# An encoder layer whose first stage is put in another order: x is transposed at once, shift and scale become columns, two engines share their sum

## Chip, cores and metric

One core of one Trainium2 chip. The time is the device time of one launch in microseconds (us), from a few runs of the same program; smaller is better. The profile is one more execution of it, taken with the hardware profiler.

## What is computed

One layer of a bidirectional encoder on 512 tokens of width 1024, all in fp32. Cut to what matters here:

```python
mod = silu(c) @ w_ada + b_ada                     # c: (1, 1024), w_ada: (1024, 6*1024)
sh_a, sc_a, g_a, sh_f, sc_f, g_f = split(mod, 6)
h = layer_norm(x) * (1.0 + sc_a) + sh_a           # (512, 1024)
proj = h @ w_in                                   # w_in: (1024, 3072): q, k, v of two head groups
o_na = neighbourhood_attention(proj, na_rpb)      # 8 heads, learned 2-D relative bias
o_diff = diff_attention(proj, t5_bias, lambda)    # 4 heads, two softmax maps, T5 bucketed bias
x = layer_norm(ALPHA * x + (1.0 + g_a) * (concat(o_na, o_diff) @ w_out), ln1)
h = layer_norm(x) * (1.0 + sc_f) + sh_f
x = layer_norm(ALPHA * x + (1.0 + g_f) * peer(h), ln2)   # 16 experts of 16384 for each of 8 heads, gathered row by row
```

## The kernel before

Five instruction streams are written by hand, one for each engine, and meet only through semaphores. SP issues all loads but the gathers. TensorE (`block.tensor`) walks through one list, `GROUPS` (function `phase_a_groups`): each group fills one of six PSUM banks in turn (`bank[g % BANKS]`), and ScalarE or VectorE evacuates it in the same order; before it fills a bank TensorE waits until the group six before has been evacuated.

The stages are:

- **First stage.** TensorE makes the table of the neighbourhood bias (`na_table`, 8 groups of a 32-row product), the T5 lines (`t5_line`, 8 groups, one for each of 4 heads and 2 halves, since one product copies a head's line to all 128 partitions) and the transposed keys (`keys_t`). VectorE normalises the four 128-token tiles of x (`normalise`: statistics, a reciprocal root on GpSimd, one subtraction and multiplication). Then it sums the first four of twelve chunks of w_ada. A chunk is 1024 rows by 512 columns (2 MB), and `sum_chunk` multiplies its eight 128-row blocks by silu(c) and adds them, which leaves a 128x512 tile; a product with a matrix of ones on TensorE adds over the partitions and copies the sum to all of them (`ada` groups). These first four chunks are shift and scale of the first sub-layer (`mods_a`). VectorE then makes h for each tile with a multiplication and an addition of 128x1024 (L763, L764), TensorE transposes it (`h_t`), and ScalarE copies it to `h_t` in SBUF.
- **Projection stage.** Six chunks of w_in, four groups of eight 128x512 products each; between them come the eight other `ada` groups. All chunks of w_ada and w_in come through a ring of five 2 MB slots in the order of `STREAM`: ada 0 to 3, proj 0, ada 4, ada 5, proj 1, and so on. `chunk_used` makes SP wait until a slot is free.
- **Attention** (48 head and tile pairs), output projection, query projection and key scores, then the **expert stage**, where GpSimd gathers the chosen experts' rows in 1024 transfers of 128 rows.

SP's order before: x, the small tables, five chunks, the rows of b_ada (`mods`), then it waits for `na_table` and writes the table to DRAM (`na_scr`), waits for the T5 lines and writes them, skewed by one element a row, to `t5_scr`; both are read back later as the bias tiles. Then come the chunks from the sixth on. Two of the small loads have elements of 4 bytes in an order that is not contiguous: c (L286) and na_rpb (L293).

Of the kernel before, what the change touches and what calls it, by code (L numbers as in the profile page):

```python
# [19 lines left out]
ALU = mybir.AluOpType  # L20
# [28 lines left out]

STREAM = [("ada", i) for i in range(ADA_FIRST)]  # L50
for _i in range(IN_CHUNKS):
    STREAM += [("proj", _i)] + [("ada", i) for i in range(ADA_FIRST + 2 * _i, min(ADA_FIRST + 2 * _i + 2, ADA_CHUNKS))]
# [49 lines left out]
ON_DVE = ("ada", "scores", "values", "out")  # L102
# [13 lines left out]
LAST_PROJ = INDEX[("proj", (STREAM.index(("proj", IN_CHUNKS - 1)), IN_CHUNKS - 1, 3))]  # L116
# [9 lines left out]
def build(nc, x, c, w_ada, b_ada, w_in, w_out, na_rpb, t5_bias, lambda_q1, lambda_k1, lambda_q2,  # L126
# [3 lines left out]
    with ctx:  # L130
# [24 lines left out]
        stats = sb("stats", [P, 2, 6])  # L155

        h_t = region_h[:, :].rearrange("p (k s) -> p k s", k=KB)
        mixed = region_h[:, :].rearrange("p (t d) -> p t d", t=TILES)
        t5_stage = region_h[:, :].rearrange("p (h j) -> p h j", h=DIFF_HEADS)
# [6 lines left out]
        t5_rep = region_qw[0:T5_BUCKETS, 5376:5376 + DIFF_HEADS * P].rearrange("p (h m) -> p h m", m=P)  # L166
# [20 lines left out]
        mods_a = misc[:, 1024:3072].rearrange("p (a d) -> p a d", a=2)  # L187
# [17 lines left out]
        c_col = small[:, 0:8]  # L205
# [18 lines left out]


# [4 lines left out]
        tables_in = sem("tables_in")  # L230
        rpb_in = sem("rpb_in")
        x_in = sem("x_in")
        rows_in = sem("rows_in")
        mods_in = [sem(f"mods_in{i}") for i in range(2)]
# [11 lines left out]
        ln2_in = sem("ln2_in")  # L246
        c_ready = sem("c_ready")
        c_exp_done = sem("c_exp_done")
# [6 lines left out]
        h_ready = sem("h_ready")  # L255
# [28 lines left out]
        def _(sp):  # L284
            sp.dma_start(x_sb[:, :, :], x[0].rearrange("(t p) d -> p t d", p=P)).then_inc(x_in, 16)
            sp.dma_start(c_col, c.rearrange("a (k p) -> p (a k)", p=P), allow_slow_non_contiguous=True).then_inc(tables_in, 16)  # L286
            sp.dma_start(na_place_sb, na_place).then_inc(tables_in, 16)
# [28 lines left out]
            for n in range(WSLOTS):  # L316
                load_chunk(n)
# [12 lines left out]
            for n in range(WSLOTS, CHUNKS):  # L330
                load_chunk(n)
# [675 lines left out]
```

## Time and profile before

| | us |
|---|---|
| median of 3 runs | 1945.46 |
| lowest and highest | 1943.44, 1948.09 |
| profiled execution, its own time | 1944.35 |
| span in the profile | 1942.6 |
| first product of the projection stage starts | 96.47 |
| last projection starts to be evacuated | 268.41 |
| expert stage starts | about 608 |

A row of the trace names engine, source line and the tiles written and read (`pair` is PSUM, `big` the large SBUF buffer in which most tiles lie, `region_v` the normalised x and later v). PE is TensorE, PEld its weight loads, DVE VectorE, ACT ScalarE, POOL GpSimd, SPq SP's DMA issues. An fp32 product is two matmul instructions in the trace, a transpose is one.

### The profile page before, as it was taken

To read this page: it belongs to the slowest core of one execution; us is meant where nothing else is said; L and a number is where in the kernel's file an instruction comes from. 1 tells how busy PE (TensorE), PEld (TensorE's weight loads), DVE (VectorE), ACT (ScalarE), POOL (GpSimd) and SP (SyncE) were. 2 spreads that over 40 slices of the span, in tenths; PEclk is the share of its full clock that TensorE was granted. 3 is DMA by queue.
4 is the path that set the end of the run, shared out by engine and by line. 5 is a ranking of instruction groups with operands and counts; after the bars stand their busy time and mean duration, and the time that the engine had idled before them with its cause. 6 is when DMAs were issued, how large, how long until landed. Compare 5 with 4: busy or idle time off the path is not lost.

```text
span 1942.6 us, 14972 instructions
## 1 busy us (share of the span) xinstructions
PE 1537.7 (79%) x4570; PEld 687.8 (35%) x4570; DVE 1178.0 (61%) x2808; ACT 388.6 (20%) x955; POOL 984.3 (51%) x1065
## 2 busy tenths in 40 slices
PE   2599999999998777777777777777777777777777
PEld 1244446655996222222222222222222222222222
DVE  1844027758801677666777766776766776676642
ACT  1100025520112111221111221111321111221111
POOL 0000000000303777777777777777777777777772
PEclk9999989999998999999999999999999999999999
DMA  4965443022504999999999999999999999999994
GB/s 139 343 249 211 131 129 74 14 109 87 196 1 155 409 409 409 409 410 409 409 410 409 407 409 408 409 402 406 407 405 404 408 405 403 410 404 409 406 409 185
DMA packets 193334, 612.95 MB, mean 316 GB/s; under 512 B 30248, under 2 KB 30632, under 8 KB 192968
## 3 DMA queue, kind: packets, MB, share of 16 engines
q0 software_dynamic: 147456, 536.94, 69.6%
q1 hardware_dynamic: 45800, 75.06, 11.9%
q8 instruction: 38, 0.62, 0.1%
q14 instruction: 40, 0.33, 0.0%
HBM read 605.77 MB, written 6.16 MB: 315 GB/s over the span
## 4 chain that ended last, share of the span: by engine, by line
PE 25%; DMA 25%; DVE 24%; POOL 15%; issue 7%; SPq 2%; ACT 1%; POOLq 0%; DVEq 0%; PEldq 0%
DMA big<-in_expert_down,expert_idx 24%; PE pair L441 22%; DVE big L926 9%; POOL big L419 8%; POOL big L410 8%; PE pair L560 2%; SPq L295 1%; DMA big<-in_expert_up,expert_idx 1%; DVE big L733 1%; PE pair L504 1%; DVE big L863 1%; DVE big L846 1%; DVE big L867 1%; DVE big L868 1%; PE pair L544 1%
## 5 line engine op out<-in xcount | busy, mean ns | idle before, releaser
L560 PE MATMUL pair<-big 128*128 128x512 f32 x2048 | 999.9, 612 | 323.1 <-DMA big<-in_expert_up,expert_idx 288.4
L926 DVE CUSTOM_DVE_ANT_0 big<-big,pair 128x1024 f32<-128x1024 f32 x512 | 611.2, 1219 | 340.8 <-DMA big<-in_expert_down,expert_idx 339.5
L560 PEld LDWEIGHTS pair<-big 128*128 128x128 f32 x2048 | 349.0, 189 | 973.3 <-issue 858.3
L410 POOL DMA_INDIRECT big<-in_expert_down,expert_idx x512 | 484.7, 947 | 300.7 <-issue 119.9
L419 POOL DMA_INDIRECT big<-in_expert_up,expert_idx x512 | 483.6, 944 | 156.9 <-issue 147.1
L441 PE MATMUL pair<-big 128*128 128x128 f32 (+3 forms) x1704 | 421.9, 415 | 21.6 <-DVE big L733 13.2
L441 PEld LDWEIGHTS pair<-big 128*128 128x128 f32 (+2 forms) x1704 | 237.2, 193 | 166.1 <-issue 147.8
L398 POOL TENSOR_SCALAR small<-small 128x1 f32<-128x1 f32 (+1 forms) x16 | 3.6, 226 | 463.6 <-DVE small L806 350.7
L636 ACT ACTIVATE big<-big 128x16 f32<-128x16 f32 x32 | 6.9, 215 | 1026.0 <-DVE big L926 1026.0
L647 ACT ACTIVATE big<-ident,big 128x128 f32<-128x128 f32 x512 | 153.0, 387 | 16.1 <-DVE big L881 16.1
L629 ACT ACTIVATE big<-pair 128x512 f32<-128x512 f32 (+1 forms) x136 | 77.9, 591 | 323.1 <-PE pair L441 227.0
L781 DVE CUSTOM_DVE_ANT_0 big<-pair,big 128x512 f32<-128x512 f32 x64 | 44.0, 687 | 75.8 <-PE pair L441 75.2
L878 DVE RECIPROCAL big<-big 128x1 f32<-128x1 f32 x32 | 5.2, 164 | 133.6 <-ACT big L638 133.6
L733 DVE SCALAR_TENSOR_TENSOR big<-big,small 128x512 f32<-128x512 f32 x84 | 63.2, 752 | 3.0
L578 ACT ACTIVATE big<-big,small 128x512 f32<-128x512 f32 x64 | 46.2, 721 | 62.3 <-DVE small L785 62.3
L441 PE MATMUL pair<-region_v,big 128*128 128x64 f32 (+1 forms) x384 | 53.7, 286 | 4.4 <-ACT big L629 3.7
L441 PEld LDWEIGHTS pair<-region_v,big 128*128 128x128 f32 x384 | 50.3, 204 | 7.4 <-issue 4.2
L754 DVE SCALAR_TENSOR_TENSOR mods<-pair,mods 128x512 f32<-128x512 f32 x8 | 5.5, 688 | 62.5 <-PE pair L441 62.5
L926 DVE DVE_READ_ACCUMULATOR2_ANT big<- 128x1 f32 x512 | 42.3, 83 | 0.0
L638 ACT ACT_TABLE_LOAD x32 | 41.1, 1283 | 0.6
L441 PE MATMUL pair<-mods,big 32*120 32x512 f32 x16 | 14.0, 1063 | 34.3 <-DMA big<-in_na_rpb 34.3
L636 ACT ACT_TABLE_LOAD x31 | 39.8, 1283 | 0.5
(111 smaller groups left out, 662.4 us busy)
## 6 DMA issues: line engine op xcount, KB each, us to landing
big<-in_w_ada SPq DMA_DIRECT2D x12, 2048.0 KB, 17.6
big<-in_w_in SPq DMA_DIRECT2D x6, 2048.0 KB, 15.5
big<-na_scr SPq DMA_DIRECT2D x8, 1024.0 KB, 10.6
big<-in_w_query SPq DMA_DIRECT2D x4, 2048.0 KB, 12.8
big<-in_expert_down,expert_idx POOLq DMA_INDIRECT x512, 11.8
big<-in_expert_up,expert_idx POOLq DMA_INDIRECT x512, 11.9
big<-in_w_out SPq DMA_DIRECT2D x2, 2048.0 KB, 10.6
x_sb<-in_x SPq DMA_DIRECT2D x1, 2048.0 KB, 7.9
```

The costliest lines, as they stand in the source:

```text
L410: nc.gpsimd.indirect_dma_start(downs[at % DOWN_SLOTS], None, expert_down[0], bass.IndirectOffsetOnAxis(expert_idx[:, at:at + 1], 0)).then_ ...
L419: nc.gpsimd.indirect_dma_start(ups[:, at % UP_SLOTS, :], None, expert_up[0], bass.IndirectOffsetOnAxis(expert_idx[:, at:at + 1], 0)).then_ ...
L441: last = nc.tensor.matmul(ps, a, b, start=(i == 0), stop=(i == len(pairs) - 1))
L560: last = nc.tensor.matmul(pair[t % 2][:, s * HALF:(s + 1) * HALF], diag[:, at % TOPK, :], ups[:, at % UP_SLOTS, s * HALF:(s + 1) * HALF], ...
L578: nc.scalar.activation(probs[:, a % 3, m, :], probs[:, a % 3, m, :], ACT.Exp, bias=max_neg[:, slot:slot + 1], accum_out=row_sum[:, slot:sl ...
L629: nc.scalar.activation(dst, ps if kind in ("keys_t", "na_table", "h_t") else ps[:, :], ACT.Copy, scale=scale).then_inc(act_evac, 1)
L636: nc.scalar.activation(gate_exps[:, head % 2, :], at_head(gate_arg, head), ACT.Exp, accum_out=gate_sum[:, head % 2:head % 2 + 1]).then_inc ...
L638: nc.scalar.activation(acts[:, head % 2, :], at_head(dots, head), ACT.Gelu).then_inc(gate_done, 1)
L647: nc.scalar.activation(diag[:, j, :], ident[:, :], ACT.Copy, scale=weights[:, head % 2, j:j + 1]).then_inc(diag_done, 1)
L733: last = v.scalar_tensor_tensor(out=acc, in0=w[:, k, :], scalar=c_exp[:, k:k + 1], in1=acc, op0=ALU.mult, op1=ALU.add)
L781: v.tensor_tensor_reduce(out=probs[:, a % 3, m, :], in0=ps[:, :], in1=bias, scale=1.0, scalar=-3.0e38, op0=ALU.add, op1=ALU.max, accum_out ...
L926: v.tensor_tensor_reduce(out=downs[slot], in0=downs[slot], in1=u_cur[:, :], scale=1.0, scalar=0.0, op0=ALU.mult, op1=ALU.add, accum_out=do ...
```

## The change

Seven things are changed together.

1. c, the first 2048 elements of b_ada and na_rpb are loaded row by row (contiguous) and transposed by TensorE (groups `cols`, `rpb_cols`); VectorE copies them out of PSUM. The row broadcasts of the lambdas and of subln move on SP's queue from before the first chunk to behind the fifth. The broadcast of 1 MB of b_ada (`mods_a`) is gone.
2. VectorE takes the statistics of all four tiles, GpSimd makes the four reciprocal roots at once, ScalarE normalises (four 128x1024 activations), and TensorE transposes the normalised x without waiting for shift and scale (28 transposes, then 4 more).
3. The first four chunks of w_ada are summed without `ada` groups in between. Of chunks 2 and 3 VectorE sums five blocks and GpSimd three (`sum_blocks`: five instructions of 128x512 a chunk). TensorE reduces a sum to columns: for each 128 columns a product with one column of ones (`mod_columns`), 24 products.
4. Shift and scale are then per-partition scalars, and h is made while it is copied out of PSUM: one instruction a block, 5 on VectorE (`h_dve`), 3 on ScalarE (`h_act`). The 128x1024 multiplications and additions are gone.
5. The T5 lines are 2 groups instead of 8 (one product holds 4 heads by 32 rows), behind the first projection; `keys_t` goes with them. The write to `t5_scr` is four DMAs from the same tile.
6. SP writes `na_scr` and `t5_scr` behind the tenth chunk, instead of ahead of the sixth. Chunks 6 to 9 now wait for `mod_summed`, which TensorE signals behind the last of the 24 products; the tenth waits for the first projection.
7. The projections come in the order 2, 5, 3, 4, 0, 1.

```diff
+IN_ORDER = [2, 5, 3, 4, 0, 1]
+ADA_ON_DVE = [KB, KB, 5, 5]
-    g = [("na_table", (j,)) for j in range(8)]
-    g += [("t5_line", (h, s)) for h in range(DIFF_HEADS) for s in range(2)]
-    g += [("keys_t", ())]
-    for n, (kind, i) in enumerate(STREAM):
-        g += [(kind, (n, i, b)) for b in range(4 if kind == "proj" else 1)]
-        if n == ADA_FIRST - 1:
-            g += [("h_t", (t, s)) for t in range(TILES) for s in range(2)]
+    g = [("cols", ()), ("rpb_cols", ())]
+    g += [("na_table", (j,)) for j in range(8)]
+    g += [("h_act" if k % 3 == 1 else "h_dve", (k,)) for k in range(KB)]
+    for n, (kind, i) in enumerate(STREAM[ADA_FIRST:]):
+        g += [(kind, (n + ADA_FIRST, i, b)) for b in range(4 if kind == "proj" else 1)]
+        if n == 0:
+            g += [("t5_line", (s,)) for s in range(2)]
+            g += [("keys_t", ())]
...
 # SP
+                if n < ADA_FIRST:
+                    sp.wait_ge(mod_summed, 1)
...
+            for n in range(WSLOTS, WSLOTS + 3):
+                load_chunk(n)
+
+            for n in range(WSLOTS + 3, WSLOTS + 5):
+                load_chunk(n)
             sp.wait_ge(act_evac, EVAC[INDEX[("na_table", (7,))]][1])
...
-            sp.wait_ge(act_evac, EVAC[INDEX[("t5_line", (DIFF_HEADS - 1, 1))]][1])
-            sp.dma_start(bass.AP(t5_scr, 0, [[D + 1, P], [P * (D + 1), DIFF_HEADS], [1, D]]),
-                         t5_stage).then_inc(t5_written, 16)
-            for n in range(WSLOTS, CHUNKS):
+            sp.wait_ge(act_evac, EVAC[INDEX[("t5_line", (1,))]][1])
+            for q in range(4):
+                sp.dma_start(bass.AP(t5_scr, q * (P // 4) * (D + 1), [[P * (D + 1), DIFF_HEADS], [D + 1, P // 4], [1, D]]),
+                             t5_line).then_inc(t5_written, 16)
+            for n in range(WSLOTS + 5, CHUNKS):
                 load_chunk(n)
...
 # GpSimd
+            def sum_blocks(n):
+
+                pool.wait_ge(w_in_slot[n], 16)
+                acc, w, k0 = pool_sum[:, n % 2, :], w_slot[n], ADA_ON_DVE[n]
+                link(nc.gpsimd.tensor_scalar(acc, w[:, k0, :], c_exp[:, k0:k0 + 1], None, ALU.mult))
+                for k in range(k0 + 1, KB):
+                    link(nc.gpsimd.tensor_scalar(pool_tmp, w[:, k, :], c_exp[:, k:k + 1], None, ALU.mult))
+                    last = nc.gpsimd.tensor_tensor(acc, acc, pool_tmp, ALU.add)
+                    if k < KB - 1:
+                        link(last)
+                last.then_inc(pool_summed, 1)
...
 # TensorE
+            def mod_columns(n):
+
+                pe.wait_ge(ada_summed, n + 1)
+                if ADA_ON_DVE[n] < KB:
+                    pe.wait_ge(pool_summed, sum(k < KB for k in ADA_ON_DVE[:n + 1]))
+                for b in range(4):
+                    last = nc.tensor.matmul(mod_ps[:, 4 * n + b:4 * n + b + 1], first_sum[:, n, b * P:(b + 1) * P],
+                                            ones[:, 0:1], start=True, stop=(ADA_ON_DVE[n] == KB))
+                    if ADA_ON_DVE[n] < KB:
+                        last = nc.tensor.matmul(mod_ps[:, 4 * n + b:4 * n + b + 1], pool_sum[:, n % 2, b * P:(b + 1) * P],
+                                                ones[:, 0:1], start=False, stop=True)
...
+                    if g == FIRST_PROJ:
+                        pe.wait_ge(act_evac, EVAC[INDEX[("h_act", (KB - 1,))]][1])
+                        pe.wait_ge(dve_evac, EVAC[INDEX[("h_dve", (KB - 2,))]][1])
...
 # ScalarE
+                if kind == "na_table" and args[0] == 4:
+                    act.wait_ge(shift_ready, 1)
+                    for t in range(TILES):
+                        nc.scalar.activation(x_norm[:, t, :], x_sb[:, t, :], ACT.Identity, bias=shift4[:, t:t + 1],
+                                             scale=rstd4[:, t:t + 1]).then_inc(norm_ready, 1)
...
 # VectorE
+            for n in range(ADA_FIRST):
+                sum_chunk(n)
+            dve.wait_ge(mod_summed, 1)
+            v.tensor_tensor(mod_cols[:, 0:KB], mod_ps[:, 0:KB], cols[:, KB:2 * KB], ALU.add)
+            v.scalar_tensor_tensor(out=mod_cols[:, KB:2 * KB], in0=mod_ps[:, KB:2 * KB], scalar=1.0,
+                                   in1=cols[:, 2 * KB:3 * KB], op0=ALU.add, op1=ALU.add).then_inc(mod_ready, 1)
...
-                    h = ln_tmp[:, t % 2, :]
-                    link(v.tensor_tensor(h, x_norm[:, t, :], mods_a[:, 1, :], ALU.mult))
-                    v.tensor_tensor(h, h, mods_a[:, 0, :], ALU.add).then_inc(h_ready, 1)
+                elif kind == "h_dve":
+                    k, = args
+                    dve.wait_ge(pe_group, g + 1)
+                    v.tensor_scalar(h_t[:, k, :], ps[:, :], mod_cols[:, KB + k:KB + k + 1], mod_cols[:, k:k + 1],
+                                    ALU.mult, ALU.add).then_inc(dve_evac, 1)
```

Where the instructions stand. The first place is SP's queue, before, from the small tables to the sixth chunk:

```order
L293 DMA big<-in_na_rpb 31x120x1 [waits ones_set]
L295 DMA big<-in_lambda_q 128x64
L295 DMA big<-in_lambda_k 128x64
L296 DMA subln<-in_diff_subln 128x128
L297 DMA big<-in_b_ada 128x2048
L313 DMA big<-in_w_ada 128x8x512 x4
L313 DMA big<-in_w_in 128x8x512
L319 DMA mods<-in_b_ada 128x4096 [waits pe_group]
L323 DMA na_scr<-big 120x64x64 [waits act_evac]
L328 DMA t_scr<-big 128x4x1024 [waits act_evac]
L313 DMA big<-in_w_ada 128x8x512 [waits ada_summed] x2
```

And the same queue after, from the first chunk to the third projection's chunk:

```order
L336 DMA big<-in_w_ada 128x8x512 x4
L336 DMA big<-in_w_in 128x8x512
L342 DMA big<-in_lambda_q 128x64
L343 DMA subln<-in_diff_subln 128x128
L345 DMA mods<-in_b_ada 128x4096 [waits pe_group]
L336 DMA big<-in_w_ada 128x8x512 [waits mod_summed] x2
L336 DMA big<-in_w_in 128x8x512 [waits mod_summed]
L336 DMA big<-in_w_ada 128x8x512 [waits mod_summed]
L336 DMA big<-in_w_ada 128x8x512 [waits pe_group]
L353 DMA na_scr<-big 120x64x64 [waits act_evac]
L359 DMA t_scr<-big 4x32x1024 [waits act_evac]
L336 DMA big<-in_w_in 128x8x512 [waits ada_summed]
```

The broadcasts have gone behind the five chunks, and the two table writes from between the fifth and sixth chunk to between the tenth and eleventh. The eleventh is the third projection's.

The second place is VectorE, before, from the last statistics to the first h:

```order
L690 TENSOR_SCALAR region_v<-x_sb,small 128x1024 [waits rstd_ready]
L731 TENSOR_SCALAR big<-big,small 128x512 [waits w_in_slot0,dve_step]
L733 SCALAR_TENSOR_TENSOR big<-big,small 128x512 [waits dve_step] x7
L731 TENSOR_SCALAR big<-big,small 128x512 [waits w_in_slot1]
L754 SCALAR_TENSOR_TENSOR big<-pair,big 128x512 [waits mods_in0,pe_group]
L754 SCALAR_TENSOR_TENSOR big<-pair,big 128x512 [waits pe_group] x2
L763 TENSOR_TENSOR big<-region_v,big 128x1024 [waits dve_evac]
L764 TENSOR_TENSOR big<-big 128x1024 [waits dve_step]
```

And after, from the T5 copy to the last block of h:

```order
L795 COPY t_rep<-big 32x128 [waits t5_in]
L800 BN_STATS stats<-x_sb 128x6 [waits x_in]
L810 SCALAR_TENSOR_TENSOR shift<-mean_var,small 128x4 [waits rstd_ready,c_ready]
L822 TENSOR_SCALAR big<-big,small 128x512 [waits w_in_slot0]
L824 SCALAR_TENSOR_TENSOR big<-big,small 128x512 [waits dve_step] x7
L822 TENSOR_SCALAR big<-big,small 128x512 [waits w_in_slot3]
L824 SCALAR_TENSOR_TENSOR big<-big,small 128x512 [waits dve_step] x4
L833 TENSOR_TENSOR mod_cols<-pair,cols 128x8 [waits mod_summed]
L854 TENSOR_SCALAR big<-pair,mod_cols 128x512 [waits pe_group,mod_ready]
L854 TENSOR_SCALAR big<-pair,mod_cols 128x512 [waits pe_group] x4
```

Normalisation, the four `ada` evacuations and the 128x1024 work on h have left VectorE; the last two sums have four instructions of L824 instead of seven, and a wait for TensorE stands between the sums and h.

## Rows read from the trace of the kernel before

**Rows 1.** Windows by stage: length, busy and count of each engine, clock, DMA, GB/s.

```profile
0.00:36.00 36.00, 1.73 (x2) 0.79 (x3) 1.03 (x5) 1.49 (x2) 0.97 (x9) 1.00 0.33 82
48.00:62.00 14.00, 14.00 (x18) 5.16 (x17) 10.96 (x19) 4.85 (x9) 2.10 (x5) 1.00 1.05 387
96.50:268.40 171.90, 171.87 (x400) 75.85 (x400) 51.16 (x72) 13.74 (x23) 0.00 (x0) 1.00 0.55 180
608.00:1942.00 1334.00, 1000.39 (x2053) 349.33 (x2051) 882.36 (x2085) 257.56 (x681) 952.95 (x1008) 0.99 1.00 398
```

**Rows 2.** Timeline of SP's queue: start, time the issue took.

```profile
7.22 25.99 SPq L295 DMA_DIRECT2D big<-in_lambda_q  x1
35.62 14.96 SPq L313 DMA_DIRECT2D big<-in_w_ada  x4
55.97 5.29 SPq L319 DMA_DIRECT2D mods<-in_b_ada  x1
61.30 0.44 SPq L323 DMA_DIRECT2D na_scr<-big  x1
62.55 20.93 SPq L328 DMA_DIRECT2D t_scr<-big  x1
```

**Rows 3.** Timeline of all engines, 12 to 97 us.

```profile
12.97 0.41 DVE L706 COPY big<-big 32x512 f32<-32x512 f32 x1 [11.97 <-DMA big<-in_sub_keys]
34.27 13.97 PE L441 MATMUL pair<-mods,big 32*120 32x512 f32 x16 [34.27 <-DMA big<-in_na_rpb]
41.12 0.22 DVE L713 CUSTOM_DVE_ANT_0 big<-big 128x64 f32<-128x64 f32 x1 [27.22 <-DMA subln<-in_diff_subln]
42.15 1.29 DVE L677 BATCH_NORM_STATS2 stats<-x_sb 128x6 f32<-128x512 f32 x2
44.98 0.81 DVE L690 TENSOR_SCALAR region_v<-x_sb,small 128x1024 f32<-128x1024 f32 x1 [1.12 <-POOL small L399]
56.53 0.49 DVE L731 TENSOR_SCALAR big<-big,small 128x512 f32<-128x512 f32 x1
57.05 5.47 DVE L733 SCALAR_TENSOR_TENSOR big<-big,small 128x512 f32<-128x512 f32 x7
84.07 0.69 DVE L754 SCALAR_TENSOR_TENSOR big<-pair,big 128x512 f32<-128x512 f32 x1 [1.63 <-PE pair L441]
96.47 104.10 PE L441 MATMUL pair<-big 128*128 128x512 f32 x242 [0.79 <-ACT big L629]
```

**Rows 4.** VectorE and ScalarE in the projection stage.

```profile
97.82 0.49 DVE L731 TENSOR_SCALAR big<-big,small 128x512 f32<-128x512 f32 x1 [3.35 <-DMA big<-in_w_ada]
124.21 0.60 ACT L629 ACTIVATE big<-pair 128x512 f32<-128x512 f32 x1 [6.27 <-PE pair L441]
153.39 0.60 ACT L629 ACTIVATE big<-pair 128x512 f32<-128x512 f32 x1 [6.27 <-PE pair L441]
```

**Rows 5.** DMA issues: KB each, median us from issue to landing.

```profile
mods<-in_b_ada SPq DMA_DIRECT2D x1, 2048.0 KB, 19.5
t_scr<-big SPq DMA_DIRECT2D x1, 2048.0 KB, 29.6
na_scr<-big SPq DMA_DIRECT2D x1, 1920.0 KB, 24.7
```

**Rows 6.** Landing of the two chunks issued at 153.4 and 153.8 us (L313).

```profile
DMA to landing us min/median/max: 7.9/10.4/12.9
```

**Rows 7.** GpSimd in the timeline.

```profile
1.30 0.28 POOL L389 TENSOR_SCALAR_AFFINE_SELECT ident<-ident 128x128 f32<-128x128 f32 x1 [0.25 <-POOL ident L388]
44.37 0.58 POOL L399 TENSOR_TENSOR small<-small 128x1 f32<-128x1 f32 x1
```

**Rows 8.** TensorE's timeline around 90 and 350 us.

```profile
92.22 1.07 PE L474 MATMUL pair<-ident,big 128*128 128x128 f32 x8 [0.45 <-DVE big L764]
348.32 1.81 PE L441 MATMUL pair<-region_v,big 128*128 128x64 f32 x8
356.31 1.00 PE L441 MATMUL pair<-region_v,big 128*128 128x64 f32 x8
```

More of the change, by code:

```diff
@@ L48 @@
 ADA_FIRST = 4
+IN_ORDER = [2, 5, 3, 4, 0, 1]
+ADA_ON_DVE = [KB, KB, 5, 5]
 STREAM = [("ada", i) for i in range(ADA_FIRST)]
 for _i in range(IN_CHUNKS):
-    STREAM += [("proj", _i)] + [("ada", i) for i in range(ADA_FIRST + 2 * _i, min(ADA_FIRST + 2 * _i + 2, ADA_CHUNKS))]
+    STREAM += [("proj", IN_ORDER[_i])] + [("ada", i) for i in range(ADA_FIRST + 2 * _i, min(ADA_FIRST + 2 * _i + 2, ADA_CHUNKS))]
 CHUNKS = len(STREAM)
@@ L101 @@
 INDEX = {g: i for i, g in enumerate(GROUPS)}
-ON_DVE = ("ada", "scores", "values", "out")
+ON_DVE = ("cols", "rpb_cols", "h_dve", "ada", "scores", "values", "out")
 def at_head(a, head):
@@ L401, in _ @@
                 n += 1
+                if n == 1:
+                    pool.wait_ge(c_ready, 1)
+                    for i in range(ADA_FIRST):
+                        if ADA_ON_DVE[i] < KB:
+                            sum_blocks(i)
             def gather_down(head, j):
@@ L461, in _ @@
+                    if s == 0:
+                        pe.wait_ge(t5_in, 32)
+                        pe.wait_ge(t5_ready, 1)
+                    last = product(ps[:, :], [(t5_rep[:, :], t5_place_sb[:, s * HALF:(s + 1) * HALF])])
                 elif kind == "keys_t":
+                    pe.wait_ge(keys_in, 16)
                     for a in range(2):
@@ L546, in _ @@
                 last.then_inc(pe_group, 1)
+                if kind == "h_dve" and args[0] == 6:
+                    for n in range(ADA_FIRST):
+                        last = mod_columns(n)
+                    last.then_inc(mod_summed, 1)
             pe.wait_ge(pe_group, len(GROUPS))
@@ L628, in _ @@
                     dst = key_scores[:, at:at + 2, :].rearrange("p h n -> p (h n)")
-                nc.scalar.activation(dst, ps if kind in ("keys_t", "na_table", "h_t") else ps[:, :], ACT.Copy, scale=scale).then_inc(act_evac, 1)
+                nc.scalar.activation(dst, ps if kind in ("keys_t", "na_table") else ps[:, :], ACT.Copy, scale=scale).then_inc(act_evac, 1)
             def front(head):
@@ L731, in sum_chunk @@
+                ks = ADA_ON_DVE[n] if n < ADA_FIRST else KB
                 link(v.tensor_scalar(acc, w[:, 0, :], c_exp[:, 0:1], None, ALU.mult))
-                for k in range(1, KB):
+                for k in range(1, ks):
                     last = v.scalar_tensor_tensor(out=acc, in0=w[:, k, :], scalar=c_exp[:, k:k + 1], in1=acc,
                                                   op0=ALU.mult, op1=ALU.add)
-                    if k < KB - 1:
+                    if k < ks - 1:
                         link(last)
```

208 lines of the change are left out of this document (122 added, 86 removed).

## The prediction

> **What bounds the kernel now.** I read the windows by stage first: they say which engine fills which stretch. In the first 36 us nearly nothing runs, TensorE 1.73 us and VectorE 1.03 us. From 96.5 to 268.4 us TensorE is busy 171.87 of 171.90 us with 400 instructions, 0.43 us each, while DMA is busy 0.55: the projection stage is TensorE's own pace. The last 1334 us are the gathers at 398 GB/s [rows 1]. No stage overlaps the one before it by more than a transfer, since attention needs the last projection and the gathers need the key scores. So what the first stage gives up moves everything behind it, and what counts is when the first projection product starts, 96.47 us now [rows 3].
>
> Then SP's queue and the timeline before 96.47, to see what makes it late. One issue, that of the first lambda broadcast behind the two loads of 4-byte elements, holds SP for 25.99 us, from 7.22 to 33.2; the chunks are issued from 35.62 on [rows 2]. VectorE waits 27.22 us for the broadcasts, and TensorE 34.27 us for na_rpb [rows 3]. After that VectorE is the chain: statistics and normalisation of four tiles from 42.15 to 56.5, four chunk sums to about 82, the last `ada` product, its evacuation at 84.07, and then the 128x1024 work on h with its transposes until TensorE starts at 96.47 [rows 3].
>
> **The new chain, step by step.** The small loads are contiguous, so SP should not be held; x, the tables and the keys are issued as now within some 5 us, and the tables landed by 12.97 [rows 3]. I take 12.6 for the moment VectorE has T5's rows and x (12 to 14). The T5 copy takes 0.3. Statistics of a tile: from 42.15 to 44.98 are 2.83, of which 1.12 is the wait for GpSimd and about 0.15 the copy of the variance, so 1.56; four are 6.2. Copy, root and the shift column add 1.5. The sums begin at 20.6.
>
> A full sum takes 0.49 and 5.47, 5.9 in all; with three of the seven additions gone (5.47 / 7 = 0.78 each), 3.6. Two of each are 19.0, which ends at 39.6. Are the chunks there? They move at 387 GB/s [rows 1], 5.4 us for 2 MB. Queued behind x and the tables (2.9 MB, landed by 12.97) they land at about 18, 23.5, 29, 34 and 39.5: each before its sum, and chunk 4, the projection's, in time.
>
> GpSimd can start at 29 and has ten instructions of 128x512. No row has one. The nearest is the 128x128 select, 0.28, which scaled by four is 1.1; the smallest is 0.58 for a power of one column [rows 7]. Ten by 0.6 to 1.4 are 6 to 14; at 1.0 it is done at 39.5, together with VectorE. From above I keep 14, which would end at 43.
>
> A second unknown is whether the two engines hinder each other while both read `big`. No row shows 128x512 work on both. Bounds: nothing, or full exclusion, in which VectorE stands still for all ten, 10 us. I take 3 us, nearer to nothing, because part of each instruction is start-up and not reading, and no row shows a slowed L733. The Trainium skill, SBUF — State Buffer, section Who interferes with whom, says that a VectorE instruction with two SBUF inputs and a GpSimd instruction that reads SBUF exclude each other for a whole instruction. By that rule the sums end near 49.5 and not at 39.6; the trace has no case of it.
>
> TensorE has transposed x by then: `na_table` takes 13.97 for 8 groups [rows 3], from about 13 to 27; ScalarE's four activations (0.60 for 512 columns [rows 4], about 1.05 for 1024) stand among its copies and end near 26; 28 transposes, 1.07 / 8 = 0.13 each at the higher clock [rows 8] and 0.27 at the lower, are at most 7.5, to 34.5. What is left behind the sums is the last chunk's eight products of one column, 16 instructions. The nearest rows are those of 64 columns, 1.81 for eight at the lower clock, 1.00 at the higher [rows 8]: 3.6 us. Then the two small VectorE instructions with their waits, 0.6, and five copies of 0.62 (between L731's 0.49 and L754's 0.69), 3.1, while ScalarE's three, with a last transpose between, take about as long. With 0.4 for semaphores: 39.6 + 3 + 3.6 + 0.6 + 3.1 + 0.4 = 50.3. Against 96.47 that is 46.2 us earlier.
>
> **What is given back.** TensorE is nearly idle from 34.5 to 50 and will probably start the projections at 1.2 GHz. The rows show both levels: 0.87 an instruction in `na_table`, 13.97 for 16, and 0.43 in the projections [rows 1, 3]; and in attention, behind a pause, the same eight instructions take 1.81 at 348.32 and 1.00 at 356.31, 8 us later [rows 8]. If the first 5 us run at half pace, 2.5 is lost (0 to 4). The two T5 lines, four instructions of 0.43, and two transposes are now in the projection stage: 2.0. The six T5 groups that disappear and the other parts of `ada` save nothing, for TensorE was waiting there. Sum: 46.2 - 2.5 - 2.0 = 41.7. The profiled execution took 1944.35, so 1902.6; the median is 1.1 above that execution and I say 1903.
>
> **The moved table writes.** They are hidden now before the projections only in part; after, they stand ahead of the third projection's chunk. Let E be the end of the first projection. SP issues the tenth chunk at E, it lands 7.9 later [rows 6]. `na_scr` landed at 61.30 + 24.7 = 86.0, the load ahead of it at 55.97 + 19.5 = 75.5: 10.5 for it. `t5_scr` landed at 62.55 + 29.6 = 92.15, 6.2 behind [rows 2, 5]; the next chunk at 97.82, 5.7 behind [rows 4]. So the eleventh chunk lands at E + 30.3. It is wanted after T5 lines and keys (2.0), two `ada` groups, the second projection and two more `ada` groups. One projection with two `ada` groups is 153.39 - 124.21 = 29.2 [rows 4], two further `ada` groups are 1.7: E + 32.9. It is in time by 2.6 us. If that cover goes, each microsecond more of the writes is one lost. The sixth to ninth chunks wait for the columns at about 46.6 and land by 70; the second projection's is wanted near 84. The order of projections changes no count.
>
> **Rivals.**
> - *Full exclusion.* One engine stands still while the other reads `big`; the sums take 10 us longer, not 3: 1909.6. For it: from 29 us on the two work on the same buffer without a pause. Against it: nothing here shows such a stop. L824 of chunks 2 and 3 decides. The rule of the Trainium skill's SBUF — State Buffer, cited above, would have it so.
> - *The eleventh chunk late.* The writes are small rows (256 bytes for `na_scr`) and `t5_scr` comes as four transfers now. If both take half as long again, 8.3 more, the stall is 5.7: 1908.3. The margin of 2.6 speaks against it.
> - *The change does not do what it says*: SP is held by something else in the small loads (rows of 124 bytes instead of 4), and the chunks stay late. If 20 of the 26 us remained, the last sum would end near 58 and not 42.6: 1918. The contiguous issue at 61.30 took 0.44 [rows 2], so this is unlikely.
> - *Slower than before.* GpSimd's sums are the one term without a near row. They decide when they end later than VectorE's. The rest of the chain behind them is 7.7, so the gain is gone if they end near 84, 5.5 us an instruction, and at 8 us each the projections start at 29 + 80 + 7.7 = 116.7, which with the 4.5 given back is 24.7 lost: 1969. The longest row is 0.58 [rows 7], a tenth of the turning point.
>
> **Chances.** The forecast, between no and half exclusion, 60 in 100 (1898 to 1907); full exclusion 19; late chunk 11; held queue 4; better than all this, with the clock up at once and no exclusion, 3 (1896); slower 3. The range reaches from 1896.5, where no exclusion and a warm start meet, to 1916, where full exclusion and the late chunk do; outside are the held queue and the slow GpSimd. A measurement of this kernel tells about 0.2%, 3.9 us, from no change: faster 0.96, same 0.01, slower 0.03.
>
> **What would show it.** Right: the chunks issued from 5 us on; first statistics near 13; sums from 20 to 40 or 50; first projection product between 47 and 58; a first projection of about 30 us with instructions of 0.85 at its head; then 0.43 without a gap up to the last projection near 227; the gathers again 1334 us long. Wrong: L824 far above 0.78 beside GpSimd; a wait of TensorE for a chunk ahead of the third projection; a product of one column above 0.25; a stretch at the lower clock that goes on through the first projection (27 us more if all of it).

## The result, and the profile after

The changed kernel took 1924.70 us, the median of 4 runs (1923.65 to 1925.15); the kernel before took 1946.45 beside it (4 runs, 1943.44 to 1948.09). The ratio is 0.9892, with a 95% interval of 0.9878 to 0.9906. So it is 21.7 us faster, where I had forecast about 42, and 1924.70 lies above my range, which ended at 1916. The profiled execution took 1924.53 us, with a span of 1922.7.

First the windows of the changed kernel: length, then busy time and count of TensorE, its weight loads, VectorE, ScalarE and GpSimd, then clock, DMA share and GB/s.

```profile
55.70:119.20 63.50, 63.44 (x142) 27.46 (x142) 25.27 (x39) 6.45 (x12) 0.00 (x0) 0.96 0.67 220
119.20:133.40 14.20, 0.00 (x0) 0.00 (x0) 0.00 (x0) 0.00 (x0) 0.00 (x0) 0.61 0.82 287
133.40:250.60 117.20, 116.48 (x264) 51.16 (x264) 26.28 (x37) 9.55 (x16) 0.00 (x0) 0.97 0.51 157
590.00:1922.00 1332.00, 1001.27 (x2048) 349.43 (x2048) 882.51 (x2085) 255.97 (x677) 951.79 (x1008) 0.99 1.00 399
```

The gathers are what they were: 399 GB/s against 398 [rows 1], and from the issue of the first gather of `expert_up` to the end of the span 1332.1 us (from 590.59), against 1332.0 before (from 610.62). The projection stage is not: 14.2 us of it are empty on all five engines. The timeline of TensorE (start, busy time, line, shapes, count, and in brackets the idle time before it with what ended it) says for what it waited:

```profile
47.94 0.56 PE L498 MATMUL pair<-big 128*128 128x1 f32 x2 [3.45 <-POOL big L433]
55.73 30.26 PE L489 MATMUL pair<-big 128*128 128x512 f32 x64 [1.93 <-DVE big L854]
85.92 1.98 PE L489 MATMUL pair<-big,t_rep 32*128 32x512 f32 x4
88.11 31.07 PE L489 MATMUL pair<-big 128*128 128x512 f32 x72
133.45 116.48 PE L489 MATMUL pair<-big 128*128 128x512 f32 x264 [14.27 <-DMA big<-in_w_in]
250.71 1.99 PE L489 MATMUL pair<-big 64*128 64x512 f32 x8 [0.78 <-ACT big L711]
```

The first projection product starts at 55.73 instead of 96.47 [rows 3], 40.7 us earlier, but the scores start at 250.71 instead of 269.15 (the corresponding eight products of before), only 18.4 earlier. The third projection waited 14.27 us for the eleventh chunk. The granted clock, 1.00 until 122 us, was 0.50 (the lower level, 1.2 GHz) from 124 to 138 us and 1.00 again from 140. After the wait 264 instructions took 116.48 us; at the 0.43 of [rows 1] they are 113.4. So the idle time cost 3.1 us more at the lower clock. With 2.8 us lost at the lower clock at the head of the first projection and 2.2 for the T5 lines and transposes these account for the 22.3 us between 40.7 and 18.4.

How SP's queue and VectorE's timeline look in the changed kernel (a queue's row gives the time that the issues took):

```profile
4.50 16.91 SPq L336 DMA_DIRECT2D big<-in_w_ada  x4
86.44 0.59 SPq L353 DMA_DIRECT2D na_scr<-big  x1
88.56 20.39 SPq L359 DMA_DIRECT2D t_scr<-big  x4
109.00 4.75 SPq L336 DMA_DIRECT2D big<-in_w_in  x1
...
14.07 0.21 DVE L795 COPY t_rep<-big 32x128 f32<-32x128 f32 x1 [9.84 <-DMA big<-in_t_bias]
22.36 0.48 DVE L822 TENSOR_SCALAR big<-big,small 128x512 f32<-128x512 f32 x1
22.88 5.48 DVE L824 SCALAR_TENSOR_TENSOR big<-big,small 128x512 f32<-128x512 f32 x7
34.72 1.49 DVE L822 TENSOR_SCALAR big<-big,small 128x512 f32<-128x512 f32 x1
36.25 4.61 DVE L824 SCALAR_TENSOR_TENSOR big<-big,small 128x512 f32<-128x512 f32 x4
41.51 4.61 DVE L824 SCALAR_TENSOR_TENSOR big<-big,small 128x512 f32<-128x512 f32 x4
```

The weight chunks are issued from 4.50 instead of 35.62 [rows 2], so the early queue is free. From 88.56 on, the issues of the four narrow table writes take 20.39 us, and behind them comes the chunk for which TensorE waits. Windows inside that stretch show how the writes move:

```profile
104.00:106.00 2.00, 2.00 (x6) 0.94 (x5) 0.00 (x0) 0.36 (x1) 0.00 (x0) 1.00 0.26 57
108.00:110.00 2.00, 2.00 (x6) 0.81 (x5) 0.00 (x0) 0.00 (x0) 0.00 (x0) 1.00 0.23 92
112.00:114.00 2.00, 2.00 (x6) 0.89 (x5) 0.00 (x0) 0.00 (x0) 0.00 (x0) 1.00 0.25 100
```

The DMA share, the mean busy share of the core's sixteen DMA engines, is a quarter, as much as four of them at full work, and they move 57 to 100 GB/s. In the edit the write at L359 had become four writes whose outermost dimension is `DIFF_HEADS`, which is 4 (I call this form narrow, and the one with 32 outermost wide); the one write of before had 128 outermost. That gave the theory for the first experiment (A in its expectation below: the form of the write makes the chunk late). Its rivals: the writes are slow whatever their form, because they share DMA with `na_scr` or with small rows; and, for the later start of the projections, GpSimd's own pace against mutual hindrance with VectorE.

### The profile page after: what moved, and what is told of

It is laid out like the page before. It is cut to its first block, busy times and chain, and to the rows that moved or that the text cites. A ratio compares the mean times of both kernels' runs of the same rounds, so it can differ in the third digit from the quotient of the medians.

```text
span 1922.7 us, 15009 instructions
## 1 busy us (share of the span) xinstructions
PE 1532.5 (80%) x4600; PEld 691.7 (36%) x4600; DVE 1166.5 (61%) x2793; ACT 387.7 (20%) x948; POOL 998.6 (52%) x1069
## 4 chain that ended last, share of the span: by engine, by line
DMA 27%; PE 25%; DVE 22%; POOL 17%; issue 7%; ACT 1%; SPq 1%; POOLq 0%; PEldq 0%; DVEq 0%
DMA big<-in_expert_down,expert_idx 23%; PE pair L489 21%; DVE big L1027 9%; POOL big L467 8%; POOL big L458 8%; PE pair L636 2%; DMA big<-in_w_in 1%; DMA big<-in_w_ada 1%; DMA big<-in_expert_up,expert_idx 1%; PE pair L576 1%; DVE big L964 1%; DVE big L947 1%; DVE big L968 1%; DVE big L969 1%; PE pair L616 1%
## 5 line engine op out<-in xcount | busy, mean ns | idle before, releaser
L489 PE MATMUL pair<-big 128*128 128x128 f32 (+2 forms) x1680 | 405.3, 409 | 23.7 <-DMA big<-in_w_in 14.3
L489 PEld LDWEIGHTS pair<-big 128*128 128x128 f32 (+1 forms) x1680 | 231.8, 193 | 158.2 <-issue 143.0
L711 ACT ACTIVATE big<-pair 128x512 f32<-128x512 f32 (+1 forms) x122 | 70.2, 589 | 314.1 <-PE pair L489 247.3
L824 DVE SCALAR_TENSOR_TENSOR big<-big,small 128x512 f32<-128x512 f32 x78 | 62.2, 797 | 2.8
L576 PE MATMUL pair<-ident,big 128*128 128x128 f32 x192 | 32.5, 294 | 4.8 <-DVE big L1055 3.5
## 6 DMA issues: line engine op xcount, KB each, us to landing
big<-in_expert_down,expert_idx POOLq DMA_INDIRECT x512, 11.9
```

The costliest lines, as they stand in the source:

```text
L489: last = nc.tensor.matmul(ps, a, b, start=(i == 0), stop=(i == len(pairs) - 1))
L576: last = nc.tensor.transpose(ps[:, k * P:(k + 1) * P], probs[:, a % 3, 0, k * P:(k + 1) * P], ident[:, :])
L711: nc.scalar.activation(dst, ps if kind in ("keys_t", "na_table") else ps[:, :], ACT.Copy, scale=scale).then_inc(act_evac, 1)
L824: last = v.scalar_tensor_tensor(out=acc, in0=w[:, k, :], scalar=c_exp[:, k:k + 1], in1=acc, op0=ALU.mult, op1=ALU.add)
```

## The experiments

Runs of a group share a chip and its runs of the kernel before. `t5_spread`, `pool_alone`, `dve_sums` and `slow_rpb` ran beside one another where the gathers move about 400 GB/s and the kernel before took 1945.38 us. All others ran on three other chips, where the gathers of every traced kernel move only about 340 to 345 GB/s, and the kernel before took 2189 to 2201 us. The stages ahead of the gathers hardly differ: the scores of `t5_spread` start at 232.35 us on the one chip and at 233.05 on another. So there the starts in the trace and the ratios count, and absolute times are compared only within a group.

### The T5 write with 32 outermost

The T5 tile's rows are interleaved (row r*4+h instead of h*32+r), so that the same bytes go to the same addresses with 32 outermost:

```diff
-                sp.dma_start(bass.AP(t5_scr, q * (P // 4) * (D + 1), [[P * (D + 1), DIFF_HEADS], [D + 1, P // 4], [1, D]]),
+                sp.dma_start(bass.AP(t5_scr, q * (P // 4) * (D + 1), [[D + 1, P // 4], [P * (D + 1), DIFF_HEADS], [1, D]]),
...
-            v.tensor_copy(t5_rep[:, :].rearrange("p (h r) -> p h r", h=DIFF_HEADS),
-                          t5_lhs.unsqueeze(2).to_broadcast([T5_BUCKETS, DIFF_HEADS, P // DIFF_HEADS])).then_inc(t5_ready, 1)
+            v.tensor_copy(t5_rep[:, :].rearrange("p (r h) -> p r h", h=DIFF_HEADS),
+                          t5_lhs.unsqueeze(1).to_broadcast([T5_BUCKETS, P // DIFF_HEADS, DIFF_HEADS])).then_inc(t5_ready, 1)
```

> The changed kernel with the lines of the four heads interleaved over the partitions (row times 4 plus head), so that each of the four writes to t5_scr has 32 rows and not 4 heads as its outermost dimension. Same 2 MB, same 4 KB rows, same place in the queue, same number of DMAs. Theory A (an outermost dimension of 4 keeps a write on 4 of the 16 DMA engines; the trace shows a DMA share of 0.25 from 104 to 114 us): the four writes take about 6 us and not 20, the wait of TensorE for the third projection's chunk goes from 14.3 us to 0 to 2, with it 3 us of low clock behind it; time 1906 to 1910. Theory B (the place of the writes in the queue and the small rows of na_scr are to blame, the prediction's margin of 2.6 us was simply too thin): na_scr is unchanged, so the wait stays above 8 us; time 1916 to 1925.

It took 1906.45 us (4 runs, 1906.33 to 1906.74) against 1945.38: 0.9804 (0.9785 to 0.9822). That is 18.3 below the changed kernel and what theory A expected. Its timeline on TensorE, and its windows over the same stretch of the table writes:

```profile
55.63 29.45 PE L489 MATMUL pair<-big 128*128 128x512 f32 x64 [1.93 <-DVE big L854]
87.21 144.37 PE L489 MATMUL pair<-big 128*128 128x512 f32 x336
232.35 1.99 PE L489 MATMUL pair<-big 64*128 64x512 f32 x8 [0.78 <-ACT big L711]
```

```profile
104.00:106.00 2.00, 2.00 (x6) 0.90 (x5) 0.00 (x0) 0.00 (x0) 0.00 (x0) 1.00 0.97 361
108.00:110.00 2.00, 2.00 (x6) 0.80 (x5) 0.00 (x0) 0.27 (x1) 0.00 (x0) 1.00 0.96 277
112.00:114.00 2.00, 2.00 (x6) 0.94 (x5) 0.00 (x0) 0.00 (x0) 0.00 (x0) 1.00 1.02 391
```

The same 2 MB in the same four transfers now fill the DMA engines (share 0.97 and 0.96 instead of 0.26 and 0.23), and 336 instructions follow one another without a gap. The projections start where they did (55.63), so all of the difference lies in the wait: the scores start 18.36 earlier in the trace and the time is 18.3 lower. How the eleventh chunk lands, first in the changed kernel, then in this one. The first line of each is the queue in the 1.1 and 1.4 us behind the chunk's issue (packets, MB, share of 16 engines); the others are issues, with KB and us to landing:

```profile
q1 hardware_dynamic: 30, 0.11, 26.6%
big<-in_w_in SPq DMA_DIRECT2D x1, 2048.0 KB, 24.3
na_scr<-big SPq DMA_DIRECT2D x1, 1920.0 KB, 18.4
```

```profile
q1 hardware_dynamic: 154, 0.56, 100.4%
big<-in_w_in SPq DMA_DIRECT2D x1, 2048.0 KB, 11.2
na_scr<-big SPq DMA_DIRECT2D x1, 1920.0 KB, 20.4
...
87.65 18.88 SPq L359 DMA_DIRECT2D t_scr<-big  x4
```

In the changed kernel the chunk was issued at 109.00 and landed 24.3 later, at 133.3. Here it was issued at 106.58 and landed 11.2 later, at 117.8. The second projection ended there at 118.3, so the chunk is in time by half a microsecond. The last row, from SP's timeline, shows that the issues of the wide writes take nearly as long as those of the narrow ones, 18.88 against 20.39. So of the 15.5 us by which the chunk lands earlier only 2.4 lie in its issue; 13.1 lie in how fast what stands ahead of it moves.

The edit changes two things at once: the number of the outermost dimension, 4 or 32, and with it the order of the addresses, one head's rows after another or the four heads in turn. The write of before, with 128 outermost and the heads in turn, was fast too (6.2 us behind `na_scr`). No run has the one without the other, so which of the two makes the narrow write slow is not shown.

### The order instead of the form

The narrow writes stay; the eleventh chunk is issued ahead of `na_scr`:

```diff
             for n in range(WSLOTS + 3, WSLOTS + 5):
                 load_chunk(n)
+            load_chunk(WSLOTS + 5)
...
-            for n in range(WSLOTS + 5, CHUNKS):
+            for n in range(WSLOTS + 6, CHUNKS):
```

> The changed kernel with its narrow T5 writes as they are, but the third projection's chunk issued ahead of the two table writes and not behind them. Theory A (the writes take 12 and 20 us whatever stands where; the wait is only for what is queued behind them): no wait ahead of the third projection; the fourth projection's chunk, wanted 62 us after the end of the first, lands 64 after it, so a wait of 0 to 4 us there; time 1907 to 1912. Theory B (the narrow write slows what moves beside it too): the third projection's chunk or the fourth's is 8 us or more late; time above 1915.

One run, 2157.33 us; the kernel before took 2189.28 there, so its time can't be held against the expected one. Its TensorE timeline, and the VectorE row that belongs to the wait:

```profile
87.33 59.39 PE L490 MATMUL pair<-big 128*128 128x512 f32 x138
150.46 1.78 PE L490 MATMUL pair<-big 128*128 128x512 f32 x3 [3.73 <-DVE big L825]
238.15 1.99 PE L490 MATMUL pair<-big 64*128 64x512 f32 x8 [0.78 <-ACT big L712]
...
137.61 0.48 DVE L823 TENSOR_SCALAR big<-big,small 128x512 f32<-128x512 f32 x1 [19.34 <-DMA big<-in_w_ada]
```

There is no wait ahead of the third projection, as theory A expected. One of 3.73 us comes at 146.7, not for the fourth projection's chunk but for VectorE's sums, which had themselves waited 19.34 us, until 137.61, for a chunk that stood behind the same writes. The scores start at 238.15, 5.8 later than with the wide writes. So it was the place in the queue behind slow writes that cost, and putting one chunk ahead of them removes the wait for that chunk and moves a smaller part of the delay one chunk further. Widening the writes removes it.

### GpSimd alone, and no GpSimd

`pool_alone` keeps VectorE off chunks 2 and 3 until GpSimd is through; `dve_sums` gives VectorE all blocks of all chunks.

```diff
             for n in range(ADA_FIRST):
+                if n == 2:
+                    dve.wait_ge(pool_summed, 2)
                 sum_chunk(n)
```

> The changed kernel, but VectorE does not begin its part of the sums of chunks 2 and 3 until GpSimd has finished all ten of its instructions, so that most of these run beside an idle VectorE (VectorE's second full sum still runs until about 34.5 us). Theory A (the two engines hinder each other: 1.26 to 2.11 us an instruction on GpSimd, 1.15 for L824 beside it instead of 0.78): behind 34.5 us GpSimd's instructions take about 0.8 to 1.2 us, and L824 is back at 0.78; GpSimd ends near 42 and not 47.8. Theory B (GpSimd's own pace is 1.3 to 2.1 us, and it is only slower than was thought): its instructions take what they took, it ends near 47.5. In both the first projection starts later than 55.7 us, since VectorE's 7.2 us follow: near 57 by A, near 62 by B.

One run, 1929.36 us; the first projection starts at 61.81, near the 62 of theory B. GpSimd in the changed kernel, then in this one:

```profile
30.39 2.11 POOL L430 TENSOR_SCALAR big<-big,small 128x512 f32<-128x512 f32 x1 [8.21 <-DMA big<-in_w_ada]
34.44 1.49 POOL L433 TENSOR_TENSOR big<-big 128x512 f32<-128x512 f32 x1
46.53 1.26 POOL L433 TENSOR_TENSOR big<-big 128x512 f32<-128x512 f32 x1
```

```profile
30.62 2.10 POOL L430 TENSOR_SCALAR big<-big,small 128x512 f32<-128x512 f32 x1 [8.30 <-DMA big<-in_w_ada]
39.14 1.56 POOL L430 TENSOR_SCALAR big<-big,small 128x512 f32<-128x512 f32 x1
45.44 1.26 POOL L433 TENSOR_TENSOR big<-big 128x512 f32<-128x512 f32 x1
...
47.26 3.11 DVE L824 SCALAR_TENSOR_TENSOR big<-big,small 128x512 f32<-128x512 f32 x4
```

With VectorE idle, a multiplication takes 1.56 and an addition 1.26, not the 0.8 to 1.2 of theory A. GpSimd ends at 46.70 instead of 47.79. Six and four of them are 14.4 us, the ten intervals between starts another 1 us; the rest of the 17.4 in the changed kernel, about 2, is hindrance by VectorE. So GpSimd was late mainly by its own pace. VectorE is the one that is hindered: four L824 take 3.11 here, 0.78 each as in [rows 3], and 4.61 beside GpSimd, 1.15 each. Chunks 2 and 3 take it 7.2 us in this run (46.74 to 53.92) and 11.4 in the changed kernel (34.72 to 46.12), and chunk 1 6.01 instead of 5.48: 4.7 us in all.

```diff
-ADA_ON_DVE = [KB, KB, 5, 5]
+ADA_ON_DVE = [KB, KB, KB, KB]
```

> The changed kernel with VectorE summing all eight blocks of all four first chunks; GpSimd sums nothing, and TensorE has 16 products of one column and not 24. By the rows of the changed kernel the sums then end at 22.4 + 4 x 5.9 = 46.0 us (GpSimd ended at 47.8), and the last products are 8 instructions and not 16, 1.7 us less. Theory A (the split bought nothing because the engines hinder each other): the first projection starts at 52 to 53 us and not at 55.7, time 2 to 4 us less, 1921 to 1923. Theory B (the split is worth what it takes off VectorE, 4.7 us): it starts at 58 to 60.

1920.56 us (4 runs, 1918.13 to 1926.32), 0.9886 (0.9862 to 0.991). The times alone can't tell it from the changed kernel, but its trace can, and it is as theory A expected (a start at 52 to 53):

```profile
45.89 1.87 PE L498 MATMUL pair<-big 128*128 128x1 f32 x8 [4.04 <-DVE big L824]
52.01 30.36 PE L489 MATMUL pair<-big 128*128 128x512 f32 x64 [1.93 <-DVE big L854]
129.61 114.95 PE L489 MATMUL pair<-big 128*128 128x512 f32 x264 [14.06 <-DMA big<-in_w_in]
245.34 1.99 PE L489 MATMUL pair<-big 64*128 64x512 f32 x8 [0.78 <-ACT big L711]
```

VectorE alone has all four sums ready by 45.9, as early as its part alone in the changed kernel (46.12) and before GpSimd's last at 47.79: what GpSimd takes off it, six L824 of 0.78 or 4.7 us, it loses again to hindrance. And only 8 instead of 16 one-column instructions are left behind them. The projections start 3.7 us earlier. The stall of 14 us stays: an earlier start moves the writes with it. GpSimd's share of the sums gained nothing here.

### The queue hold put back

The old element-wise load of `na_rpb` (3720 elements of 4 bytes) is added ahead of the first chunk; everything else is the changed kernel.

```diff
+            sp.dma_start(old_rpb, na_rpb[0].rearrange("h r c -> c (h r)"), allow_slow_non_contiguous=True).then_inc(old_in, 16)
```

> The changed kernel with one load more: na_rpb once again as before the change, element by element (3720 elements of 4 bytes), into a spare corner that nobody reads, ahead of the first chunk. Theory A (the load of 4-byte elements held SP's queue for 26 us, and its removal is the larger part of the gain): SP is held again for 20 to 26 us, the chunks land that much later, the first projection starts at 70 to 80 us, time 1940 to 1950. Theory B (the queue was held by the broadcasts behind it, and the gain came from the shorter chain on VectorE): the first projection starts within 3 us of 55.7.

One run, 1941.58 us, as theory A expected. SP's queue, TensorE, and VectorE's first sum:

```profile
4.81 38.37 SPq L340 DMA_DIRECT2D big<-in_w_ada  x4
...
76.53 30.12 PE L493 MATMUL pair<-big 128*128 128x512 f32 x64 [1.93 <-DVE big L858]
...
41.16 0.49 DVE L826 TENSOR_SCALAR big<-big,small 128x512 f32<-128x512 f32 x1 [18.71 <-DMA big<-in_w_ada]
```

The four chunk issues take 38.37 instead of 16.91, the first projection starts 20.8 later, and the scores start at 269.35, where those of the kernel before start (269.15). VectorE has its statistics as early as in the changed kernel and then waits 18.71 us for the first chunk, until 41.16. So late chunks alone would take back half of the 40.7 us by which the projections start earlier. No run splits the other half, 19.9 us. The rows of the two kernels say where the 40.7 lie, though not by which edit: VectorE's statistics start at 14.21 instead of 42.15 [rows 3], 27.9 earlier; from there to the first sum it is 8.2 us instead of 14.4; and from the first sum to the first projection 33.4 instead of 39.9. So the shorter sums and the columns in place of the 128x1024 work gave 6.6. Of the 21.7 gained in the end, this one run puts 16.9 on the queue, while the four runs of the changed kernel lie 1.5 us apart and the seven of the kernel before 8.

### Both repairs together, and the T5 copy out of the way

`spread_dve` joins the wide write with VectorE's sums; `spread_one` leaves GpSimd one chunk; `early_stats` is `spread_dve` with the T5 copy, which in the changed kernel waits for its 512-byte rows until 14.07, moved behind the statistics.

> The two edits t5_spread and dve_sums together. If they are independent terms of one sum, their savings add: the first projection at 52.0 us (3.7 before 55.7), no wait for the third projection's chunk; time 1906.45 - 3.7 = 1902.8, range 1901 to 1905. If VectorE's share mattered elsewhere, it stays at 1906.

> As spread_dve, but GpSimd sums three blocks of chunk 2, and nothing of chunk 3, so that it cannot be the last. Theory A (what GpSimd takes over it gives back by slowing VectorE: in the changed kernel VectorE lost 4.7 us beside its ten instructions, 0.47 for each): 3 x 0.78 = 2.35 less and 5 x 0.47 = 2.35 more, the first projection starts at 52.0, as in spread_dve; time 1902 to 1904. Theory B (only GpSimd's own pace was the matter, since it ended last): it starts at 49.7; time 1900.5.

> As spread_dve, but VectorE copies T5's values behind the statistics and not ahead of them. In the changed kernel x had landed at 10.4 us and VectorE began the statistics at 14.2, behind the 512-byte load of t5_bias, which landed at 14.1. Theory A (that wait is on the chain): the statistics begin at 10.5, the sums with the first chunk's landing near 19.5 instead of 22.4, the first projection starts at 49 to 50, time 1899 to 1901. Theory B (the chunks' landing takes over as the limit from the first): no more than 1 us.

They ran beside one another, the kernel before at 2189.28: `spread_dve` 2148.37 (2145.62 to 2150.47), 0.9811 (0.9794 to 0.9827); `spread_one` 2151.16 (2148.20 to 2154.07), 0.9822 (0.9805 to 0.9839); `early_stats` 2146.31 (2142.89 to 2150.80), 0.9808 (0.9787 to 0.9829). The times overlap, and the chip's slower gathers leave nothing to hold against the absolute times expected. The traces order them: the first projection starts at 51.47, 52.62 and 48.99, the scores at 228.67, 230.33 and 226.05. The 51.47 is what the two savings give together (52.0 expected). Of `spread_one`, VectorE's two kinds of instruction beside GpSimd and alone, and of `spread_dve` the first sum:

```profile
34.71 1.49 DVE L822 TENSOR_SCALAR big<-big,small 128x512 f32<-128x512 f32 x1
36.23 4.30 DVE L824 SCALAR_TENSOR_TENSOR big<-big,small 128x512 f32<-128x512 f32 x4
40.45 0.48 DVE L822 TENSOR_SCALAR big<-big,small 128x512 f32<-128x512 f32 x1
...
21.57 0.48 DVE L822 TENSOR_SCALAR big<-big,small 128x512 f32<-128x512 f32 x1
```

`spread_one` starts its first projection 1.15 us later than `spread_dve`, but 0.70 of this is that its T5 rows landed later and its sums began at 22.27 instead of 21.57. What is left for the shared chunk is 0.45 us: it gains nothing, as theory A expected, and costs next to nothing. Of `early_stats`, the wait that now stands first:

```profile
10.31 1.29 DVE L797 BATCH_NORM_STATS2 stats<-x_sb 128x6 f32<-128x512 f32 x2 [6.22 <-DMA x_sb<-in_x]
19.10 0.49 DVE L822 TENSOR_SCALAR big<-big,small 128x512 f32<-128x512 f32 x1 [0.53 <-DMA big<-in_w_ada]
```

The statistics start as soon as x is there, and the sums at 19.10 instead of 21.57, now held for 0.53 us by the first chunk itself. What it buys is 2.5 us at the first projection (48.99 against 51.47), as expected by theory A.

Three repeats on one chip, and `early_stats` once more on another, were to separate the versions by time:

> t5_spread again, so that the three versions are timed on one chip (the last comparison ran where the gathers of every kernel, the one before the change too, took some 200 us longer, and its scatter of 5 us hid differences of 3). 1906.5, range 1904 to 1909.

> spread_dve again. Its trace gave 51.5 us for the first projection and 228.7 for the first scores, against 55.6 and 232.4 in t5_spread. If the terms add: 1902.8, range 1901 to 1905. Against it: 1906, if the end does not follow the first stage.

> early_stats again. Its trace gave 49.0 us for the first projection and 226.05 for the first scores, 2.6 before spread_dve. If the end follows: 1900.2, range 1898 to 1903. Against it: no less than spread_dve.

> early_stats a third time, for its absolute time beside the kernel before the change where the gathers run at their usual 398 GB/s. From its traces: first scores at 226.05 us, 6.3 before t5_spread's 232.35, whose time was 1906.45: 1900.1, range 1898 to 1903, a ratio of 0.976 to 0.978. If the chip is again one with slow gathers, a ratio of 0.980 to 0.982.

The first three against 2200.63, in the same order: 2163.93 (2163.11 to 2166.66), 0.9839 (0.9821 to 0.9856); 2160.79 (2158.18 to 2165.63), 0.9821 (0.9802 to 0.9839); 2159.39 (2154.64 to 2164.89), 0.9807 (0.9791 to 0.9824). Then once more `early_stats` on its own: 2158.64 (2156.71 to 2161.96) against 2200.78, 0.9800 (0.9783 to 0.9818). In these traces the scores start at 233.05, 228.93, 227.00 and 225.44. So all three beat the kernel before by 37 to 43 us. The chips were again ones with slow gathers, so the absolute times expected were not tested; the ratio expected for this case, 0.980 to 0.982, came. The medians of these repeats follow the traces, but 3 to 5 us between the versions is about what the runs scatter. The lowest absolute time measured is that of `t5_spread`, 1906.45. What `early_stats` takes where the gathers run at 398 GB/s was not measured; 1906.45 less the 232.35 - 226.05 = 6.3 of the traces, about 1900, is an estimate.

## Why the prediction was wrong, by its own steps

**Right.** The gain comes from the freed queue and, with 6.6 us, from the sums by columns, and the gathers keep their length. The tail behind the sums was put at 7.7; it is 47.94 to 55.73, 7.8, with one-column instructions that follow one another every 0.21 us (3.5 for sixteen, 3.6 predicted) and copies of 0.74 (3.7 for five, 3.1 predicted). The cold start: 64 instructions took 30.26 us, which at 0.43 are 27.5, so 2.8 against 2.5. T5 lines and transposes: 2.2 against 2.0.

**The step that failed** is the sentence "`t5_scr` landed at 62.55 + 29.6 = 92.15, 6.2 behind". I took the 6.2 us from the write of before and carried it to writes of another shape. From it came "the eleventh chunk lands at E + 30.3", against a need at E + 32.9. E was about 85.9. The tenth chunk landed at E + 8.0 (7.9 predicted) and `na_scr` 10.9 behind it, at 104.8 (10.5 predicted): both as predicted. Behind `na_scr` the T5 writes and the chunk took together 28.5 us, 104.8 to 133.3, and not 6.2 + 5.7 = 11.9. With the wide form `na_scr` landed at 105.9, the last T5 write at 111.6 and the chunk at 117.8: 11.9, the predicted sum, as 5.7 and 6.2. So the order of the queue and the price of 2 MB were right, and the pattern of the changed write was not read. The mechanism was my second rival, "the eleventh chunk late", to which I gave 11 in 100 and a size of 8.3 us for both writes together, since I saw small rows and four transfers as its cause. `t5_spread` has both, and no wait. Behind `na_scr` the chunk lost 16.6 us, the stall was 14.3 and not 5.7; and the second stretch at the lower clock, 3.1 us behind the stall, stood in no case of mine. The range reached to 1916 by adding that short stall to full exclusion. (Its lower end is a slip: no exclusion and a warm start give 1902.6 - 3 - 2.5 = 1897.1 and not 1896.5. Nothing hangs on it.)

**The GpSimd term was mis-sized.** I took "at 1.0" from a 128x128 select, inside bounds of 0.6 to 1.4. Measured alone it is 1.56 or 1.26, 1.44 in the mean, just outside. The sums ended at 47.8 and not 42.6: +5.2, nearly all of the +5.4 at the first projection. But GpSimd's pace is not all of it. VectorE's own share ends at 46.1, so 3.5 of the 5.2 would have come with a faster GpSimd that hinders it as much, and only the last 1.7 are GpSimd's being last. VectorE started 1.8 later (22.36 against 20.6, of which 1.5 is the wait for the T5 rows until 14.07 and the rest GpSimd's root), and lost 4.7 instead of 3 to GpSimd. The Trainium skill, SBUF — State Buffer, section Who interferes with whom, was cited for full exclusion. By it the two would never work at once, and VectorE would stand still for the 14.4 us of GpSimd's own work; the runs show 4.7. So there is interference where the rule has it (L824 reads two inputs in SBUF), but not for whole instructions: the first L824 of chunk 2 ran from 36.25 to 37.31, inside a multiplication of GpSimd that ran from 36.03 to 37.64. The Trainium skill's GPSIMD Engine Reference, section on elementwise cycle accounting, has an addition of 2048 columns at 4497 ns; a quarter of it, 1.12 us, would have been an estimate for 512 columns, nearer to the measured 1.26 than my 1.0 from the select.

**The sum with measured terms**: 1902.6 + 5.4 (later start) + 14.3 (wait) + 3.1 (clock behind it) = 1925.4, against 1924.53 of the profiled execution. The 0.9 left over are small differences, the largest in attention: the scores start 18.4 us earlier, the first gather of `expert_up` 20.0 earlier, which no run explains.

## What to carry to other kernels

When a diff touches an access pattern and not only the place of a transfer, cost it as a new transfer: here a DRAM write with 4 outermost ran at 57 to 100 GB/s, and in the same windows the queue with 32 outermost at 277 to 391. A transfer with 2.6 us of margin is no hidden one, and a missed one costs its lateness and a stretch of TensorE at the lower clock behind it (3.1 us here). And work shared with GpSimd bought nothing here: VectorE was spared 4.7 us of sums, lost 4.7 to hindrance, and TensorE then waited for GpSimd's slower part. It bought nothing in `spread_one` either, where GpSimd was through at 39.2, long before VectorE. So ending early is not enough; what the second engine costs the first has to be set against what it takes over.

## What the runs showed of the hardware that was not expected

- A DRAM write whose pattern has 4 outermost kept the DMA share at 0.23 to 0.26; reordered to 32 outermost, 0.96 to 1.02. Which engines take which part was not looked into, nor whether the number or the order of the addresses decides.
- 128x512 in fp32 on GpSimd alone: multiplication by a column 1.56 us, addition 1.26; beside VectorE up to 2.11 and 1.49 (`pool_alone` and the changed kernel). The multiplication is the slower one.
- VectorE's L824 goes from 0.78 to 1.15 in the mean of four beside GpSimd, and L822 from 0.48 to at most 1.49: both engines slow down, and neither stops for a whole instruction of the other.
- A wait of TensorE of about 14 us ahead of 264 instructions cost 3.1 us at the lower clock behind it in the changed kernel and 2.8 in `pool_alone`, but 1.5 in `dve_sums` (114.95) and `slow_rpb` (114.97). So 3.1 holds for this run and not for every such wait.
- A 512-byte load issued at 3.47 behind 2 MB of x landed 10.6 us later, at 14.07, after x itself (issued at 2.02, landed 8.4 later).
- The gathers ran at about 400 GB/s on one chip and at about 340 to 345 on three others, where the kernel before took 2189 to 2201 us instead of 1945. For `t5_spread`, traced on both kinds, the start of the scores moved only from 232.35 to 233.05. Whether it is the chip or what else ran beside it is not shown.
